# Two hybrid decoder layers on one core: weight homes and the order of output products rearranged, last down weights in five column pieces, last combination and gates earlier

## What is computed

```python
for l in range(2):
    mix = hybrid_mixer(x, w_in[l], w_ret_o[l], w_dsa_o[l], w_out[l])
    h = layer_norm(4 ** 0.25 * x + mix, ln1_g[l], ln1_b[l])
    ffn = hierarchical_moe(h, router_grp_w[l], ..., w_gate[l], w_up[l], w_down[l])
    x = layer_norm(4 ** 0.25 * h + ffn, ln2_g[l], ln2_b[l])

def hybrid_mixer(x, w_in, w_ret_o, w_dsa_o, w_out):
    rq, rk, rv, rg, aq, ak, av, iq, ik, iw, gr, ga = split(x @ w_in)   # 9800 columns
    ret = retention(rotary(rq), rotary(rk), rv, rg)                  # 4 heads, 256 x 2048
    att = dsa_attention(rotary(aq), rotary(ak), av, rotary(iq), rotary(ik), iw)  # 256 x 1024
    merged = sigmoid(gr) * (ret @ w_ret_o) + sigmoid(ga) * (att @ w_dsa_o)
    return merged @ w_out

def hierarchical_moe(h, ...):      # 4 groups of 8 experts, top-1 group, top-2 experts in it
    y = for each token and each of its 2 experts e:
            gate * ((silu(h @ w_gate[e]) * (h @ w_up[e])) @ w_down[e])
    # w_gate, w_up: 1024 x 512, w_down: 512 x 1024 for each of 32 experts of each layer
```

## Time and profile before

| what | us |
|---|---|
| median of 3 runs | 1599.21 |
| lowest, highest | 1599.19, 1601.15 |
| profiled execution, first to last instruction | 1597.9 |
| TensorE busy | 1302.9 (82%) |
| VectorE busy | 619.6 (39%) |
| ScalarE busy | 394.1 (25%) |
| queue of the weights, share of 16 engines' span | 81.3% |
| bytes read | 522.53 MB |

### The profile page before, as it was taken

One profiled execution on the slowest core, in us unless ns is written; L12 is line 12 of the kernel. 1 busy time (PEld: TensorE's weight loads), 2 busy tenths in 40 slices (PEclk: granted clock), 3 DMA queues, 4 the chain that ended last, 5 costly groups with the idle time before them and its releaser, 6 DMA issues. The chain is left out here.

```text
span 1597.9 us, 21422 instructions
## 1 busy us (share of the span) xinstructions
PE 1302.9 (82%) x8690; PEld 882.5 (55%) x8690; DVE 619.6 (39%) x1065; ACT 394.1 (25%) x458; POOL 0.2 (0%) x4
## 2 busy tenths in 40 slices
PE   9999999999756656657799999999997556556667
PEld 8998889995312212212298988899943122212212
DVE  6788676655100100100287876865541001000102
ACT  3334734333100000001143357343320000000011
POOL 0000000000000000000000000000000000000000
PEclk9999999999978877878899999999999778788779
DMA  8455446689999999999964454366999999999996
GB/s 305 166 194 190 163 159 216 246 351 424 426 429 427 428 428 427 428 427 428 404 223 164 159 211 170 121 247 233 397 427 426 427 424 428 425 429 427 429 425 276
DMA packets 98903, 524.60 MB, mean 328 GB/s; under 512 B 5504, under 2 KB 9984, under 8 KB 71184
## 3 DMA queue, kind: packets, MB, share of 16 engines
q1 hardware_dynamic: 98080, 523.10, 81.3%
q10 hardware_dynamic: 752, 0.50, 0.1%
HBM read 522.53 MB, written 1.05 MB: 328 GB/s over the span
## 5 line engine op out<-in xcount | busy, mean ns | idle before, releaser
L1057 PE MATMUL psum<-ring,aqT 128*32 128x512 f32 x1440 | 261.9, 707 | 114.0 <-PEq L1045 114.0
L1823 DVE TENSOR_TENSOR w_low<-ring,w_high 128x2048 fp32r<-128x2048 f32 (+2 forms) x108 | 239.8, 2260 | 70.8 <-DVEq L1822 69.4
L1331 ACT ACTIVATE w_high<-ring 128x2048 fp32r<-128x2048 f32 (+2 forms) x108 | 198.7, 1887 | 194.8 <-ACTq L1327 178.4
L1057 PE MATMUL psum<-spare,aqT 128*32 128x512 f32 x256 | 131.0, 701 | 96.3 <-PEq L1158 96.3
L2059 DVE TENSOR_TENSOR qk<-psum,qk 128x512 f32<-128x512 f32 x16 | 11.1, 692 | 481.6 <-DVEq L2058 481.6
L1057 PEld LDWEIGHTS psum<-ring,aqT 128*32 128x32 f32 x1440 | 66.9, 128 | 213.2 <-issue 213.2
L1057 PE MATMUL psum<-rv,tmp 128*32 128x512 f32 x240 | 123.1, 703 | 69.8 <-PEq L1185 69.8
L734 PE MATMUL psum<-x_high,w_high 128*128 128x256 f32 x512 | 146.8, 287 | 0.0
L734 PE MATMUL psum<-x_high,w_low 128*128 128x256 f32 x512 | 143.3, 280 | 0.0
L734 PE MATMUL psum<-x_low,w_high 128*128 128x256 f32 x512 | 143.2, 280 | 0.0
L637 PE MATMUL psum<-w_high,x_high 128*128 128x512 f32 (+2 forms) x352 | 138.7, 394 | 0.0
(11 more groups left out here) (285 smaller groups left out, 2301.4 us busy)
## 6 DMA issues: line engine op xcount, KB each, us to landing
ring<-in_w_gate_dram SPq DMA_DIRECT2D x56, 2048.0 KB, 33.0
ring<-in_w_in_dram SPq DMA_DIRECT2D x34, 2048.0 KB, 7.9
ring<-in_w_up_dram SPq DMA_DIRECT2D x28, 2048.0 KB, 21.8
spare<-in_w_up_dram SPq DMA_DIRECT2D x14, 2048.0 KB, 14.3
rv<-in_w_down_dram SPq DMA_DIRECT2D x12, 2048.0 KB, 31.1
rg<-in_w_down_dram SPq DMA_DIRECT2D x12, 2048.0 KB, 35.5
x_xT<-in_w_down_dram SPq DMA_DIRECT2D x12, 2048.0 KB, 39.9
ring<-in_w_down_dram SPq DMA_DIRECT2D x12, 2048.0 KB, 29.0
```

The lines of the kernel that those rows point to most:

```text
L1057: mm = nc.tensor.matmul(bank[s, :], lhs[:, c, s], w[:, k, n * NB:(n + 1) * NB], start=(c == 0), stop=(c == chunks - 1))
L1331: nc.scalar.activation(half_tile(high, i % HIGH, w, b), half_tile(ring, i % RAW, w, b), ACT.Copy).then_inc(high_ready, 1)
L1823: V.tensor_tensor(half_tile(low, i % RAW, w, b), half_tile(ring, i % RAW, w, b), half_tile(high, i % HIGH, w, b).bitcast(f32), ALU.subtrac ...
```

## The change

It computes the same. What it does:

- Homes: `h` no longer has memory of its own; its two rows lie in `tmp` and in `x`'s first row, and `grT` lies beside `xT` (`xT_sums`). `x`, `sig`, the last half ring slot and the table lie in one piece (`joint`). There are 25 homes. The table home takes half of a matrix of the second quad (`load_second`), issued behind tile gr0; the first quad's 24 units have the other 24.
- Order: the stream has ret00, ret01, ret10, ret11 before dsa0, dsa1 (tiles 20 to 25), the jobs RO0x to RO1y come before DO0 and DO1, and `EARLY` and `FIRST` are new. VectorE and ScalarE follow that order, with the split of out1's first half on ScalarE ahead of `merged_split_high(0)`.
- Norm parameters are issued by ScalarE behind `first_gathered` and lie in `aqT` as 32 rows of 128.
- Last quad: combination of the quad before and transposition of the gates stand between gate and up, with 8 short products that keep TensorE working, instead of behind up. The last down weights come as chunk 2 left, chunk 3 left, chunk 2 right (256 KB each), chunk 3 columns 512 to 767, chunk 3 columns 768 to 1023 (128 KB each), 20 loads instead of 12, and the right columns are multiplied, copied and combined as two pieces of 256.

```diff
-OUT_TILES = ["dsa0", "dsa1", "ret00", "ret01", "ret10", "ret11", "out0", "out1"]
+OUT_TILES = ["ret00", "ret01", "ret10", "ret11", "dsa0", "dsa1", "out0", "out1"]
...
-EARLY = [(10, "spare0", "rg0"), (11, "spare1", "rg0"), (23, "table", "gr0"), (16, "rv1", "dsa0"),
-         (2, 10, "ret00"), (1, "stage", "ret01"), (3, 11, "ret10"), (18, "rg0", "out1"),
-         (22, "qk0", "out1")]
-FIRST = [(6, 2, "ret11"), (0, "qk1", "mid"), (7, 3, ""), (19, "rg1", ""), (17, "rv0", "rv"),
-         (8, 4, "out00"), (12, 6, ""), (4, 0, "out10"), (14, 8, ""), (9, 5, "out01"),
-         (13, 7, ""), (5, 1, "out11"), (15, 9, ""), (20, "x1", "x1"), (21, "x0", "x0")]
+EARLY = [(10, "spare0", "rg0"), (11, "spare1", "rg0"), (16, "rv1", "ret00"),
+         (2, 10, "ret10"), (1, "stage", "ret11"), (18, "rg0", "dsa1"), (22, "qk0", "dsa1"),
+         (0, "qk1", "out0"), (19, "rg1", "out0")]
+FIRST = [(6, 2, "dsa1"), (3, 11, "mid"), (7, 3, ""), (17, "rv0", "rv"), (8, 4, "out00"), (12, 6, ""),
+         (4, 0, "out10"), (14, 8, ""), (21, "sums", ""), (9, 5, "out01"), (13, 7, ""), (5, 1, "out11"),
+         (15, 9, ""), (20, "xT", "xT"),
+         (23, "x1_sig", "x1_sig")]
...
-PLACES = [5, 0, 1, 2, "spare", 3, 4, None, "rv", "rg", "x", 5]
+PLACES = ["u11_table", 0, 1, 2, "spare", 3, 4, None, "rv", "rg", "xT_sums", "x1_sig_u11"]
...
+                    if name == "gr0":
+                        sp.wait_ge(table_free, 1).then_inc(table_free, -1)
+                        load_second(l * NE + QUAD, 1)
...
                 used(0)
-                load(e, 0, 0)
+                sp.wait_ge(outside_in["table"], 16).then_inc(outside_in["table"], -16)
+                load_second(e, 0)
+                load(e, 1, 3, (1,))
...
+                left, third, fourth = (slice(lo, lo + size) for lo, size, _ in LAST_COLUMNS)
...
                 landed(0)
-                for n in range(2):
-                    portion(FC - 2, n)
+                portion(FC - 2, 0)
                 landed(1)
                 portion(FC - 1, 0).then_inc(y_full[0], 1)
-                pe.wait_ge(tg_copied, 1).then_inc(tg_copied, -1)
                 pe.wait_ge(y_copied[0], 1).then_inc(y_copied[0], -1)
-                combine(0, (0,), last=True)
+                combine(left, (0,), last=True)
                 landed(2)
+                portion(FC - 2, 1)
+                portion(FC - 2, 2)
+                combine(left, (1,), last=True)
+                landed(3)
                 portion(FC - 1, 1).then_inc(y_full[1], 1)
-                combine(0, (1,), last=True)
+                landed(4)
+                portion(FC - 1, 2).then_inc(y_full[1], 1)
+                pe.wait_ge(y_copied[1], 1).then_inc(y_copied[1], -1)
+                combine(third)
+                pe.wait_ge(y_copied[1], 1).then_inc(y_copied[1], -1)
+                combine(fourth, last=True)
...
+                if last:
+                    outputs_copied()
+                    for n in range(2):
+                        combine(slice(n * NB, (n + 1) * NB))
+                    turn_gates()
+                    pe.wait_ge(tg_copied, 1).then_inc(tg_copied, -1)
+                    stay_warm(8, bank_u)
                 arrived(1, 0, landed)
...
-                load_params(l)
                 router_weights(l)
                 for i in range(21, LAST - 1):
                     split_high(i)
+                split_high(LAST - 1)
+                split_high(LAST, (0,))
                 merged_split_high(0)
-                split_high(LAST - 1)
-                split_high(LAST)
+                split_high(LAST, (1,))
                 merged_split_high(1)
...
                 first_gathered()
+                load_params(l)
...
-                gated("RO0x", 0)
-                free("RO0x")
-                gated("RO0y", 2)
-                free("RO0y")
+                gated("RO1x", 4)
+                gated("RO1y", 6)
+                split_low(25)
+                gated_attention(slice(0, 4), take("DO0"))
+                free("DO0")
                 merge(0)
-                split_low(25)
+                split_low(LAST - 1)
                 merged_rest(0)
-                split_low(LAST - 1)
                 split_low(LAST, (0,))
```

More of the change, by code:

```diff
@@ L337, in build @@
         start_last = sem("start_last")
-        last_in = [sem(f"last_in{n}") for n in range(3)]
+        last_in = [sem(f"last_in{n}") for n in range(len(LAST_PARTS))]
         table_free, stage_free = sem("table_free"), sem("stage_free")
@@ L349, in build @@
         router_in = sem("router_in")
-        place_in = {v: sem(f"place_in_{v}") for v in dict.fromkeys(PLACES) if v is not None}
-        apart_in = [outside_in["qk0"], outside_in["table"]]
+        place_in = {v: unit_in[2 * v] for v in range(RING - 1)}
+        place_in |= dict(zip((*ENDS, "spare", "rv", "rg", "xT_sums"), (unit_in[UNITS - 1], *(
+            outside_in[v] for v in ("x1_sig", "spare0", "rv0", "rg0", "xT")))))
+        apart_in = [outside_in["qk0"], unit_in[UNITS - 2]]
         later_in = [apart_in[half] if m == APART else None if half else place_in[PLACES[m]]
@@ L462, in load, with load_second @@
                              ).then_inc(place_in[PLACES[stage * QUAD + n]], 16)
+            def load_second(e, half):
+                u = half * QUAD
+                landed = outside_in["table"] if half else place_in[PLACES[0]]
+                sp.dma_start(later_quad[u], unit(e, u)).then_inc(landed, 16)
             def used(*halves):
@@ L1019, in spread @@
             def spread(row, bank):
-                return nc.tensor.matmul(bank, ident[0:8, row:row + 1].broadcast_to((8, P)),
-                                        param_rows, start=True, stop=True)
+                for c in range(NB // P):
+                    one = ident[0:4 * KC, row * NB // P + c:row * NB // P + c + 1]
+                    mm = nc.tensor.matmul(bank[:, c * P:(c + 1) * P], one.broadcast_to((4 * KC, P)),
+                                          param_rows, start=True, stop=True)
+                return mm
             def spread_first():
@@ L1161, in experts @@
                 quad_half([bank_u], xgT, KC, 1, 1, tiles).then_inc(up_full, 1)
-                if not first:
+                if not (first or last):
                     outputs_copied()
@@ L1173, in experts @@
                 mm.then_inc(hidT_full, 1)
-                if not first:
+                if not (first or last):
                     for n in range(2):
-                        combine(n)
-                pe.wait_ge(gpicked, 1).then_inc(gpicked, -1)
-                for t in range(TT):
-                    mm = nc.tensor.transpose(bank_u[:, t * P:(t + 1) * P], gpick[:, t, :], ident)
-                mm.then_inc(tg_full, 1)
+                        combine(slice(n * NB, (n + 1) * NB))
+                if not last:
+                    turn_gates()
                 arrived(2, 0, landed)
```

229 lines of the change are left out of this document (127 added, 102 removed).

## The result

| | kernel before | changed kernel |
|---|---|---|
| median of 9 runs each, us | 1599.25 | 1602.93 |
| lowest, highest | 1599.12, 1602.65 | 1599.51, 1606.85 |
| profiled execution: span | 1597.9 | 1597.7 |

The ratio after to before is 1.002, with a 95% interval of 1.0011 to 1.0029. The change costs 0.2%; the forecast had 0.5% gained. The profiled execution is the fastest of the nine, and two further ones of the same program had spans of 1600.4 and 1599.8. Each of the three is the fastest of its series (1599.51, 1602.14 and 1601.82 us beside medians of 1602.93, 1605.87 and 1605.38), so what the median loses beyond that stands in none of them.

What follows compares the result with a forecast made beforehand. Expert weights on the full DMA queue were taken to set each layer's end. Per layer 2.46 + 0.3 + 1.05 = 3.8 us, two layers 7.6: 1597.9 - 7.6 = 1590.3, with 1.3 to the median 1591.6; range 1587 to 1596.

Steps and rivals of the forecast that it cites:

- The stall: Before each layer's first output block, TensorE waits 1.65 us for the merged half, and all later issues move by that.
- a late out1: Tile out1 held up by some tenths behind the units issued after out0, delaying TensorE one for one: 0.15 us allowed.
- One more home: Table home takes half a second-quad matrix at gr0, so one unit less is owed after the first pass: 2.46 us per layer.
- the reorder: Mixer's new output-product order and earlier loads: gain capped at 2.1 us, less 1.65 and 0.15, so 0.3 us per layer.
- ten units against seven: Units out by the issue of out1, after against before; the three extra are 7.4 us, not all to be gained.
- the engines never ran dry: Reading of the earlier trace from 326 us on: the DMA engines always had work, but by 2 us only.
- The cap: Limit on the gain from earlier loads: 2.1 us of work ahead of the unit issued at 357.48.
- "no stall" rival: Merged split gets its turn before out1's half, or out1 lands early enough: 5.6 us per layer, 1588.0; chance 0.15.
- The last quad: End of each layer: 3.5 us behind the last byte instead of 5.25, last byte 0.7 later; net 1.05 us per layer.
- The parameter rows: Norm parameters loaded by ScalarE behind the first gather, into the full stretch: nothing on the path, spreads 0.5 us longer.
- the slower rival: Parameter rows wait behind queued weights and TensorE stands at the spreads some 25 us: 19 us per layer, 1629; chance 0.05.
- Signs that were to show it: Profile: 1.6 us idle before the first output block, 370 GB/s from 303 to 326, a dip behind, landings 2.5 to 3 sooner.

Runs made afterwards that it cites:

- early merge: Changed kernel with ScalarE's merged split of the first half moved ahead of the split of out1's first half: 1597.13 and 1597.66 us.
- experiment 5: Changed kernel with the units into rg0, qk0, qk1 and rg1 issued later: 1605.50 us; the same with the early merge: 1605.29 us.
- experiment 3: Kernel before with ScalarE's merged split behind the split of out1's first half and VectorE's rest behind out0's low split: 1605.84 us.

## Why the forecast was wrong

**The stall: right in place, its price too low.** 1.65 us a layer were forecast; 1.6 to 2.1 came in layer one and 2.5 to 2.6 in layer two. What it costs at the landings is the difference between the early merge and the changed kernel: 3.2 less 0.4 in mixer 1 and 2.3 less -2.4 in mixer 2 (means of two and three pages), 2.8 and 4.7 us. In layer two this is the stall of 2.6, lengthened by the late landing, and 1.5 us of slow clock (first output product to first logits 22.1 us, 20.6 elsewhere). I had allowed 0.15 us for a late out1: in the first page it lands 0.14 us later than before in layer one (7.93 for 7.79) and 1.26 later in layer two (8.98 for 7.72). And the length isn't the price: in experiment 5 stalls of 1.4 and 2.8 us cost next to nothing, since no bytes were lost behind them. (The 1.5 us that my sum gives the new units to start is shown by no row; in the trace of before the first packets follow their issue at 303.22 by 1.04 us.)

**One more home: the step that failed.** It was booked at 2.46 us on top of the reorder. The count of "ten units against seven" by out1's issue already held it. And the earlier trace rows, read as "the engines never ran dry" from 326 on, say by themselves that a home has no worth of its own: if the queue is never dry in the stretch, only bytes moved ahead of it shorten it. Experiment 5 shows it: a 25th home with one unit fewer ahead of the stretch is 5 us slower.

**The cap: right in kind, wrong in place.** I read it at 357.48 (2.1 us of work ahead). In the changed kernel the queue ran dry earlier, between 332 and 344, since what bridged that time before had been pulled ahead. The right sum is 7.3 us for three units, less the dry time: 3.2 and 2.3 us are left without the stall. (From 326 to 356 us the early merge moves 1.4 MB or 3.4 us less than the kernel before, of which its DMA share shows 2.1 us as idle; the rest goes in stretches that look full and move fewer GB/s.) The forecast had 2.1 + 2.46 = 4.56 for that case, so the "no stall" rival was 1.3 to 2.3 us a layer too good as well.

Put together, the two mixers were to gain 5.5 us. The home takes 4.9 from that, the cap gives 1.3 (5.5 in place of 4.2), the stall with the late out1 takes 3.9 (7.5 in place of 3.6): -2.0, which is the mean of the three pages. The medians lie 3.7 to 6.2 us above the kernel before, and what they lose beyond the pages stays open.

**The last quad: 1.05 us a layer forecast, nothing in the medians.** The five pieces took 0.46 us more in layer two (10.85 from the last 1024 KB to the last piece, 10.39 before) and 0.7 in layer one, as forecast; the estimate by the Trainium skill (DMA: Bandwidth & Descriptors, section Measured), some 2 us more, did not come. Behind the last byte, 3.5 us were forecast. The last piece of layer two was issued at 1577.30 (KB, us to landing) and landed at 1584.67:

```profile
joint<-in_w_down_dram SPq DMA_DIRECT2D x1, 128.0 KB, 7.4
```

TensorE's last combinations and the last statistics behind it:

```profile
1586.06 1.97 PE L1140 MATMUL psum<-qk,aqT 128*128 128x256 f32 x8 [0.25 <-PEq L1186]
...
1587.63 1.30 DVE L1752 BATCH_NORM_STATS2 stat<-psum 128x6 f32<-128x512 f32 x2 [1.49 <-PE psum L1140]
```

That is 4.3 us (5.2 before): 1.1 of products and not 0.6, because those of chunk 3's columns 512 to 767, landed at 1583.31, waited behind a combination of the left half; and 1.3 of statistics and not 0.73, since the right halves of both rows of tokens are complete only at the end, and both stand on VectorE behind it. In layer one the same chain took 3.9 us in the changed kernel and 5.0 in the kernel before with the new last quad, where 5.1 stood before. The other two pages of the changed kernel have 5.3 and 4.3 us in layer one, 5.0 and 4.4 in layer two: what is won behind the last byte, less the 0.5 to 0.7 of the pieces, is -0.9 to 0.6 us a layer.

**The parameter rows: no effect, as forecast.** ScalarE issues the first of the four loads at 373.93, and TensorE goes into the spreads without a gap:

```profile
373.93 0.54 ACTq L1511 DMA_DIRECT2D aqT<-in_ln_g_dram  x1
...
386.10 4.65 PE L1054 MATMUL psum<-aqT,joint 32*128 32x128 f32 x32
```

All packets of the loads' queue fall between 377 and 380 us (packets, MB, share), the last at 379.98:

```profile
q10 hardware_dynamic: 64, 0.02, 2.4%
```

6.0 us from issue to landing in the full stretch, 5.6 in the half idle mixer. The unit of weights issued just ahead of them, at 373.51, landed at 383.7. With that the slower rival is out, and the round-robin between queues, which the forecast took from the Trainium skill (DMA: Bandwidth & Descriptors, section Queues, rings and completion order), agrees with the trace. The spreads take 4.65 us for 3.69, inside the margin.

**Signs that were to show it.** The idle time at the first output block, the GB/s of 303 to 326 and the dip behind it came. The landings from 400 us on came 1.1, 0.6 and -0.4 us sooner, not 2.5 to 3. No change and a rise of the time were given 0.06 each. The mechanism in the text, a wait at 338 in each layer, was enough for it, had its price been read by the time it leaves the queue dry and not by its length.

**Open.** The changed kernel's medians stand 3.4 to 3.7 us above its profiled executions, and experiment 3 loses in the median 2.4 us more than in its page. The traces at hand don't show such a run. From 1146 to 1162 us, in layer two, the changed kernel and the early merge move 364 and 374 GB/s at a DMA share of 0.96 to 0.97, where the kernel before moves 416; with about one unit in the queue, its engines may run out one by one. No experiment tried that.

## What to carry to other kernels

Where a DMA queue bounds a stretch, count the bytes moved ahead of it, once; a further buffer, or an earlier load, is worth what it adds to that, less every moment at which the queue behind it runs dry. Before an operation is put behind one that waits for a transfer, ask what stands behind it on the next two engines: here one line's place on ScalarE was worth 8 us, more than the whole of the rest, and at most 0.8 us in a kernel whose queue stayed full behind it. An edit that is right and one that undoes it can come in one change, and the median then says neither; test them apart.

## What the runs showed of the hardware

**Instruction transfers delay a tile.** In the 14 traces of the kernel before, the changed kernel and the first twelve experiments, 428 tiles of 2048 KB went out with nothing queued ahead of them, from 200 to 1200 us. In 284 no packet of the instruction queue q8 fell between 1 us behind the issue and 0.5 us ahead of the landing: the median from issue to landing is 7.9 us. In 144 one did, and it is 9.0. The packet has 16 KB and holds one of 16 engines for about 1 us. The Trainium skill (Runtime: NRT & Kernel Launch, section Instruction fetch mechanics) has each engine fetch its program in blocks of 16 KiB over its own DMA queue and calls the cost mostly hidden; the size agrees with the trace, the cost here is 1.1 us on the tile beside it. Adding instructions at one place moves all such packets behind it, so a change can lengthen a wait hundreds of microseconds away.

**The clock behind a stall.** In 14 stalls of 1.4 to 2.8 us at the first output block (seven pages, two layers each), the first products behind it came at half pace, at the lower of the two clock levels (granted clock 0.72 to 0.81 of full speed over the 6 us around them), in five: in all four of 2.5 us and more, and once behind 2.08 us. Behind stalls of 1.4 to 2.06 us it was never seen, nor in the four where identity products filled the first part. Each time the first logits came 22.1 to 22.2 us behind the first output product, 20.6 elsewhere: 1.5 us.
